# The mixer's channel norm among the output products, in another order

## What is computed

```python
def conformer_conv_mixer(val, gate, conv_w, conv_b, gn_g, gn_b):
    y = val * sigmoid(gate)
    y = causal_depthwise_conv(y, conv_w) + conv_b        # width 31
    y = y.reshape(B, S, 8, 64)
    y = layernorm(y, gn_g, gn_b)                          # over each group of 64 channels
    return silu(y.reshape(B, S, 512))

y_a = spatial_gating_mixer(gelu(u), gelu(v), ...)
y_b = conformer_conv_mixer(val, gate, ...)
y = concatenate([rmsnorm(y_a, out_norm_a_g), rmsnorm(y_b, out_norm_b_g)], -1)
x = x + gate1 * (y @ w_out)
h2 = modulate(rmsnorm(x, norm2_g), shift2, scale2)       # then the feed-forward part
```

## Time and profile before

| | us |
|---|---|
| median of 3 runs | 761.37 (760.92 to 764.42) |
| span of the profiled execution | 762.0 |
| TensorE matmul busy | 702.2 (92%) |
| VectorE busy | 361.2 (47%) |
| ScalarE busy | 325.4 (43%) |
| moved by the transfers | 211.44 MB, 277 GB/s on average |

### The profile page before, as it was taken

One profiled execution on the slowest core, in us unless ns is written; L12 is line 12 of the kernel. 1 busy time (PEld: TensorE's weight loads), 2 busy tenths in 40 slices (PEclk: granted clock), 3 DMA queues, 4 the chain that ended last, 5 costly groups with the idle time before them and its releaser, 6 DMA issues.

```text
span 762.0 us, 13133 instructions
## 1 busy us (share of the span) xinstructions
PE 702.2 (92%) x5455; PEld 555.6 (73%) x5456; DVE 361.2 (47%) x718; ACT 325.4 (43%) x690; POOL 61.1 (8%) x70
## 2 busy tenths in 40 slices
PE   5889899989999999999999999997999999868886
PEld 3686677887999999999978777786765555434452
DVE  3458967636544555544489589443431111111011
ACT  2347535646444444433467895757331111001011
POOL 0400002000000002000000028162000000000000
PEclk9789999999999999999999999999999999989899
DMA  9997978419666755444754336458889999999996
GB/s 338 353 406 298 412 282 301 159 56 348 232 239 230 247 190 173 167 138 141 234 167 165 125 122 218 166 221 327 311 347 421 422 420 420 421 420 420 422 407 214
DMA packets 76707, 211.44 MB, mean 277 GB/s; under 512 B 7463, under 2 KB 34245, under 8 KB 62822
## 3 DMA queue, kind: packets, MB, share of 16 engines
q1 hardware_dynamic: 75602, 209.91, 73.2%
q0 software_dynamic: 800, 0.63, 0.5%
q10 hardware_dynamic: 244, 0.03, 0.0%
HBM read 209.51 MB, written 1.05 MB: 276 GB/s over the span
## 4 chain that ended last, share of the span: by engine, by line
PE 65%; DMA 11%; DVE 11%; ACT 6%; SPq 5%; issue 2%; ACTq 0%; DVEq 0%
PE ps L1976 9%; PE ps L1977 9%; PE ps L1978 9%; PE ps L2705 6%; SPq L458 4%; PE ps L1989 4%; PE ps L1990 4%; PE ps L1991 4%; DMA ring<-in_expert_w_gate_dram 4%; DMA ring<-in_expert_w_up_dram 4%; DVE YT L1343 3%; DVE ring_low L1227 3%; PE ps L2670 3%; PE ps L2747 2%; DMA ring<-in_w_in_dram 2%; PE ps L2716 2%
## 5 line engine op out<-in xcount | busy, mean ns | idle before, releaser
L1227 DVE TENSOR_TENSOR ring_low<-ring,HI 128x1024 fp32r<-128x1024 f32 (+1 forms) x119 | 142.0, 1237 | 28.6 <-ACT HI L713 28.6
L713 ACT ACTIVATE HI<-ring 128x1024 fp32r<-128x1024 f32 (+1 forms) x135 | 133.6, 1057 | 26.6 <-DMA ring<-in_w_in_dram 26.6
L1976 PE MATMUL ps<-AH,HI 128*128 128x256 f32 x320 | 90.1, 281 | 0.4 <-DVE Z L1494 0.4
L1978 PE MATMUL ps<-AH,ring_low 128*128 128x256 f32 x320 | 89.6, 280 | 0.0
L1977 PE MATMUL ps<-AL,HI 128*128 128x256 f32 x320 | 89.4, 280 | 0.0
L2705 PE MATMUL ps<-ring,ZM 128*32 128x256 f32 x880 | 70.1, 416 | 11.1 <-DMA ring<-in_expert_w_up_dram 7.4
L1976 PE MATMUL ps<-HI,AH 128*128 128x512 f32 (+1 forms) x176 | 70.4, 400 | 2.2 <-DVE ring_low L1227 1.0
L1977 PE MATMUL ps<-ring_low,AH 128*128 128x512 f32 (+1 forms) x176 | 68.0, 386 | 0.0
L1989 PE MATMUL ps<-AH,HI 128*128 128x256 f32 x192 | 58.4, 304 | 7.3 <-DVE AL L1313 5.7
L1976 PEld LDWEIGHTS ps<-AH,HI 128*128 128x128 f32 x320 | 60.1, 188 | 3.1 <-issue 2.5
L1978 PE MATMUL ps<-HI,AL 128*128 128x512 f32 (+1 forms) x160 | 61.3, 383 | 0.0
(11 more groups left out here) (393 smaller groups left out, 1276.6 us busy)
## 6 DMA issues: line engine op xcount, KB each, us to landing
ring<-in_expert_w_up_dram SPq DMA_DIRECT2D x28, 1024.0 KB, 23.1
ring<-in_expert_w_gate_dram SPq DMA_DIRECT2D x27, 1024.0 KB, 26.2
ring<-in_expert_w_down_dram SPq DMA_DIRECT2D x24, 1024.0 KB, 22.2
ring<-in_w_ffn_in_dram SPq DMA_DIRECT2D x20, 1024.0 KB, 6.5
ring<-in_w_in_dram SPq DMA_DIRECT2D x18, 1024.0 KB, 6.2
ring<-in_ada_w_dram SPq DMA_DIRECT2D x16, 1024.0 KB, 9.2
ring<-in_w_ffn_out_dram SPq DMA_DIRECT2D x11, 1024.0 KB, 7.3
ring<-in_ada_w_dram SPq DMA_DIRECT2D x16, 512.0 KB, 10.7
```

Of the source, the lines that this page charges most:

```text
L713: act(HI[:, (i + 1) % UNITS, 0:w], W.view(name)[:, o:o + w], ACT.Copy).then_inc(s_hi, 1)
L1227: tt(W.low(name)[:, o:o + w], W.view(name)[:, o:o + w], HI[:, (i + 1) % UNITS, 0:w].bitcast(F32), ALU.subtract).then_inc(s_lo, 1)
L1976: mm(dst, lh, rh, start=start, stop=False)
L1978: return mm(dst, ll, rh, start=False, stop=stop)
```

## The change

ScalarE: the split of out1's second unit (`hi_to(io + AHEAD)`) goes ahead of the two squares `GQ`; the copies of `VM` go between them; two of the three splits that followed go ahead of the group norm's root. VectorE: one low part goes ahead of the group norm's reciprocal; after CV has been scaled and a low part written, a new instruction adds the squares of swish's tiles 2 and 3 to those of 0 and 1 (`s_gn` 5), so that TensorE has two tiles to add up in place of four; `rows_scaled` goes ahead of `columns` and `scales`. TensorE: the group sums come after tile 4 of product 1, the group spread ahead of product 2, the sums of swish's squares after tile 3 of product 3 with two tiles, their spread after tile 6; `ada(3, 0)` goes ahead of product 4, and the following ones move up by one place.

```diff
 ScalarE
             hi_to(ik + 3 + AHEAD)
+            hi_to(io + AHEAD)
             for h in range(2):
                 ac.wait_ge(s_gn, h + 1)
                 act(GQ[:, 2 * h:2 * h + 2, :], CV[:, 2 * h:2 * h + 2, :], ACT.Square).then_inc(s_sqs, 1)
-            hi_to(io + AHEAD)
+                if h == 0:
+                    ac.wait_ge(s_un, S.end["kv_v1"])
+                    for t in range(NT):
+                        act(VM[:, t, :], ps[(2, 6)[t]][:, :], ACT.Copy).then_inc(s_vm, 1)
+            for i in (1, 2):
+                hi_to(io + i + AHEAD)
             rooted(RGS, ps[3][:, 0:16], SUM_G)
             warm(ACT.Silu)
-            ac.wait_ge(s_un, S.end["kv_v1"])
-            for t in range(NT):
-                act(VM[:, t, :], ps[(2, 6)[t]][:, :], ACT.Copy).then_inc(s_vm, 1)
-            for i in (1, 2, 3):
-                hi_to(io + i + AHEAD)
+            hi_to(io + 3 + AHEAD)
 VectorE
+            lo_to(io + 1 + AHEAD)
             recip(RGS, SUM_G)
-            for i in (1, 2):
-                lo_to(io + i + AHEAD)
+            lo_to(io + 2 + AHEAD)
             for h in range(2):
                 ve.wait_ge(s_gmp, 2 + h + 1)
                 tt(CV[:, 2 * h:2 * h + 2, :], CV[:, 2 * h:2 * h + 2, :], tiles(ps[(3, 7)[h]][:, :], 2), ALU.mult).then_inc(s_gn, 1)
             lo_to(io + 3 + AHEAD)
+            ve.wait_ge(s_sqs, SQ_B + 2)
+            tt(SQY[:, 0:2, :], SQY[:, 0:2, :], SQY[:, 2:4, :], ALU.add).then_inc(s_gn, 1)
             recip(RTS[2], SUM_B)
+            rows_scaled(YB, 4, OB, ps[2][:, 256:512], RB_B)
             columns(3, 6, C2[:, B1 + 16:B1 + 32])
             scales(1, colv[:, 2, 0:8], C2[:, N2:N2 + 8], 3)
-            rows_scaled(YB, 4, OB, ps[2][:, 256:512], RB_B)
 TensorE (group_sums and groups_spread are the loops that stood after k == 1 and k == 2)
             for k in range(4):
...
+                if k == 2:
+                    groups_spread()
                 for m in range(8):
                     ins = projected(k, m, k == 0 and m % 2 == 0, False)
-                ins.then_inc(s_un, 1)
+                    if m == 7:
+                        ins.then_inc(s_un, 1)
+                    if k == 1 and m == 4:
+                        group_sums()
+                    if k == 3 and m == 3:
+                        te.wait_ge(s_vm, 2)
+                        te.wait_ge(s_gn, 5)
+                        for i in range(2):
+                            added_up(2, SQY[:, i, :], i, 2)
+                    if k == 3 and m == 6:
+                        spread(2, 256, 2, SUM_B)
...
-            for k in range(4):
-                te.wait_ge(s_sqs, SQ_B + k // 2 + 1)
-                if k == 0:
-                    te.wait_ge(s_vm, 2)
-                added_up(2, SQY[:, k, :], k, 4)
             columns(3, 6)
-            spread(2, 256, 2, SUM_B)
+            ada(3, 0)
...
-            ada(3, 0)
+            ada(3, 1)
...
-            ada(3, 1)
+            ada(3, 2)
             spread(6, 256, 3, SUM_FF)
-            for k in range(2, 5):
+            for k in range(3, 5):
                 ada(3, k)
```

More of the change, by code:

```diff
@@ L2255, in projected, with group_sums, groups_spread @@
                 return halves(tile_of(WOB, m), h, l, AH[:, k, :], AL[:, k, :], start, stop)
+            def group_sums():
+                for ct in range(4):
+                    te.wait_ge(s_sqs, SQ_G + ct // 2 + 1)
+                    for t in range(NT):
+                        ins = mm(ps[3][:, 8 * t + 2 * ct:8 * t + 2 * ct + 2], GQ[:, ct, P * t:P * t + P], blk[:, 0:P:64],
+                                 start=True, stop=True)
+                ins.then_inc(s_sum, 1)
+            def groups_spread():
+                te.wait_ge(s_rr, SUM_G)
+                for ct in range(4):
+                    for t in range(NT):
+                        x = 256 * (ct % 2) + P * t
+                        for g in range(2):
+                            c = 8 * t + 2 * ct + g
+                            ins = mm(ps[(3, 7)[ct // 2]][64 * g:64 * g + 64, x:x + P], RGS[:, c:c + 1].to_broadcast([P, 64]),
+                                     ident[:, :], start=True, stop=True)
+                    if ct % 2:
+                        ins.then_inc(s_gmp, 1)
             for k in range(4):
```

## The result

| | before | changed |
|---|---|---|
| median of 20 runs | 761.59 us (759.69 to 768.38) | 759.19 us (757.53 to 763.91) |
| span of the profiled execution | 762.0 us | 756.0 us |
| TensorE matmul busy | 702.2 us | 695.7 us |

The account below looks back on a forecast made before the run. Bound: waits on two chains, leaving TensorE holes of 1.56 and 1.57 us. Product 5 moves from 161.46 to 158.4, 3.05 us; span 762.0 becomes 758.95, less 0.63 gives 758.3 us, range 755.8 to 761.8.

Parts of the forecast that it names:

- The chain: Group sums through swish and its squares to product 5 of the output projection: that product starts 3.05 us earlier.
- Rival D: New waits before the group sums or swish's sums outlast their cover; a 1.5 us slip leaves 2.2 gain, 759.1; chance 0.10.
- From the spread to product 4: On TensorE: spread 0.71, eighth tile 0.48, columns 0.60, ada(3,0) 0.93; product 4 at 155.4.
- VectorE's side: VectorE from the spread to the low part product 5 needs: 4.09 + 0.37, then 1.27, ending at 158.4.
- What stays: Behind the last spread, one ada fewer: taken as 0, with 0.93 us kept as the upper end.
- rival E: The missing ada counts if TensorE limits the feed-forward start: up to 0.93 us more gain, 757.4; chance 0.12.
- From the trace to the time: Whole kernel: changed span 758.95, minus the 0.63 by which the earlier median lay below its span, gives 758.3.
- B: Experts' transfers set the end from an unmoving start, giving the shift back: 761.4, or 759.9 if half; chance 0.14.
- C: Granted clock falls in two more stretches where TensorE is the bound, costing 3.4 us: 761.7; chance 0.06.
- The drain of the table load: On ScalarE after the group norm's root: about 1.38 us by the skill page, which would leave about 2.4 gain.

Follow-up runs that it names:

- the second comparison: The changed kernel run again without any edit, against the kernel before: ratio 0.9929 (0.9900 to 0.9957), 5.4 us less.

## Why the prediction was right

The forecast was 758.3 us and 3.05 us of gain; measured are 759.19 and 4.4 (2.8 to 5.9), of which the trace accounts for 3.60 in the stage. Point by point, counted from the product of `blk` at 138.56 in the kernel before:

| step | predicted | measured |
|---|---|---|
| group sums start | 2.55 | 2.63 |
| group spread starts | 5.5 | 5.57 |
| product 2 starts | 7.4 | 7.46 |
| CV scaled until | 8.2 | 8.27 |
| add of squares until | 11.2 | 11.28 |
| sums of squares start | 11.9 | 11.81 |
| their spread starts | 14.1 | 13.76 |
| product 4 starts | 16.8 | 16.09 |
| product 5 starts | 19.85 | 19.30 |

**The chain was right.** The covers were thin and held: 0.22 us before the group sums (the square ended at 139.93, the sums began at 140.15; 0.14 predicted), 0.53 before the sums of the squares (0.7), 0.4 before their spread (0.5). Rival D didn't happen.

**The steps that were mis-sized** are those behind product 2, all to the same side. The sums with 8 passes take 0.81, not 0.95, and three tiles 1.14, not 1.23: 0.38 together with the 0.13 by which the sums start early. From the spread to product 4 I added 2.72 (0.71, 0.48, 0.60, 0.93) and measured 2.33 (0.36, 0.45, 0.53, 0.99), because for the spread above all I took the duration of a group where the step to the next start was wanted; the last matmul of a group runs on under the next group. On VectorE's side I had 4.09 + 0.37 = 4.46 from the spread to the low part and measured 4.26: `columns` and `scales` cost 0.28 (155.54 - 155.26), as the low part starts 0.08 after the scale, and YB's scaling starts 0.65 behind the start of the spread, not 0.75. The run with the low part first agrees, with 0.27. VectorE's side set product 5, as a near tie, with 0.11 us of hole; 0.38 before the spread and 0.20 on VectorE make the 0.55, but for rounding.

**What stays** was right where I took 0: the moved `ada` is worth nothing (its own run), and rival E with it.

**From the trace to the time** was wrong in its reason, and that the median came within 1 us of 758.3 is in part luck. I set the profiled span 0.63 above the median. In the changed kernel the time of the profiled execution was 757.78 at a span of 756.0, and in all runs of which both are known the time lies 1.7 to 1.9 above the span. So the profiled execution of the kernel before took about 763.8, above its median and not below its span. It did little harm, since what I took off the median was a difference between marks. But no difference between marks gives that of the medians, which is 2.40 here and 6.4 in the second comparison: of all times measured, 43 of 76 of the kernel before lie above 763.5, and 3 of 31 of the changed kernel.

**The rivals.** B is out by the delay of TensorE, and by the 200.3 to 201.6 us from the experts' first matmul to the end in every trace. C, the clock, was the right thing to look at with the wrong sign: in this stage it took 1.3 us in one of three traces of the kernel before and nothing in the two of the changed one, while falls elsewhere come and go in both. Why the ratio gives 0.8 us more than the 3.6 stays open; 3.6 lies within its interval, and the means of the same runs differ by 3.67. The fall in the holes would give it the right sign; the run with filled holes is too blunt to show it. None of the three traces of the kernel before is of an execution below 762 us, where 31 of its 76 times lie, so how these pass the stage isn't known.

**The drain of the table load** that the Trainium skill ("ScalarE: Activation LUTs", What ACT_TABLE_LOAD costs) adds to a switch is not seen here either: the root ends at 142.30, the load starts at 142.32, and swish started when CV was ready.

## What to carry to other kernels

A wait of one engine can be the order of another: here 3.6 us lay in work of ScalarE and VectorE that was placed on the chain (copies, splits) though both had idle time just before it, and the new order paid in full only when all three engines changed together. Work out a moved sequence from the starts of neighbouring groups, not from their durations, and check how much cover each new wait has. For an effect of 0.5%, compare marks counted from an event ahead of the change: here they repeat to 0.02 us until the next fall of the clock, some 250 us on, where whole times scatter by 9.

## What was not expected

- TensorE's granted clock fell behind holes of 1.57 and 2.27 us (0.87 and 0.83 over 10 us), for 1.3 and 1.7 us of time, and did not behind one of 3.26. Near 400 us it fell with TensorE busy all the time, to 0.74 over 20 us in one trace, and stayed at 1.00 in another of the same kernel.
- 28 transposes in a row took 0.109 us each; four between other work took 0.53, so 0.13 each.
- A pass of 256 columns follows the last after 0.12 us at the full clock and 0.21 us, not 0.24, at the half one.
